# Tails of four tiles instead of three, and where the second half of their first tile stands, in one decoder layer

## The reference, cut to what matters

```python
y = sigmoid(gate_a) * y_a + sigmoid(gate_b) * y_b
h = y @ w_out                                   # output projection
x = layer_norm(alpha * x + h, ln1_g, ln1_b)
qry = x @ w_q                                   # query projection, then top-k over keys
...
hid = gelu(einsum('cd,chkd->chk', x, u_tab[expert]))
h = einsum('chk,chkd->cd', gate * hid, v_tab[expert])   # value projection
x = layer_norm(alpha * x + h, ln2_g, ln2_b)
```

## Time and profile before

| | |
|---|---|
| median of 3 runs | 1098.83 us (1098.72 to 1099.35) |
| profiled execution | 1099.08 us |
| its span | 1097.3 us |
| PE busy | 1081.6 us, 99% |
| DVE, ACT, POOL busy | 70%, 51%, 16% |
| DMA queue of SP | 181.30 MB, 48.7% of 16 engines |

### The profile page before, as it was taken

How to read it: one execution, slowest core, us unless ns; L and a number is a source line. 1 busy time by engine, 2 the same in 40 slices (tenths; PEclk the granted TensorE clock), 3 DMA queues, 4 the chain that set the end, 5 groups by cost and what they waited for, 6 DMA issues and landing times.

```text
span 1097.3 us, 19861 instructions
## 1 busy us (share of the span) xinstructions
PE 1081.6 (99%) x6760; PEld 969.3 (88%) x6760; DVE 773.4 (70%) x1403; ACT 559.2 (51%) x903; POOL 177.5 (16%) x118
## 2 busy tenths in 40 slices
PE   8999999999999999999999999999999999999996
PEld 6888888678999999999999999998888888888885
DVE  4457657387999868889998777765555555555556
ACT  4347544564344555555556545545554455455553
POOL 2040002203000002223334555520000000000001
PEclk9999999999999999999999999999999999999998
DMA  7554344253445554444444443445565655555553
GB/s 280 190 194 155 134 157 150 96 173 129 159 166 180 185 179 155 156 163 160 153 154 153 142 146 134 137 153 193 198 208 204 205 193 191 191 191 191 192 193 112
DMA packets 52711, 186.48 MB, mean 170 GB/s; under 512 B 6320, under 2 KB 6704, under 8 KB 52672
## 3 DMA queue, kind: packets, MB, share of 16 engines
q1 hardware_dynamic: 50864, 181.30, 48.7%
q0 software_dynamic: 944, 3.15, 0.8%
q10 hardware_dynamic: 864, 1.57, 0.4%
HBM read 184.94 MB, written 1.05 MB: 169 GB/s over the span
## 4 chain that ended last, share of the span: by engine, by line
PE 92%; DVE 3%; DMA 2%; ACT 2%; POOL 1%; issue 1%; POOLq 0%; SPq 0%; DVEq 0%; ACTq 0%
PE ps L1172 17%; PE ps L1174 17%; PE ps L1173 17%; PE ps L1499 10%; PE ps L1500 10%; PE ps L1501 10%; PE ps L1460 5%; DMA raw<-w_tiles_in 1%; PE ps L1224 1%; ACT whi L462 1%; DVE wlo L726 1%; PE ps L1426 1%; PE ps L1300 1%; PE ps L1311 0%; PE ps L1316 0%
## 5 line engine op out<-in xcount | busy, mean ns | idle before, releaser
L726 DVE TENSOR_TENSOR wlo<-raw,whi 128x1024 fp32r<-128x1024 f32 x341 | 421.4, 1237 | 258.7 <-ACT whi L462 256.6
L462 ACT ACTIVATE whi<-raw 128x1024 fp32r<-128x1024 f32 x343 | 363.2, 1060 | 303.9 <-DMA raw<-w_tiles_v 167.8
L1172 PE MATMUL ps<-ahi,whi 128*128 128x256 f32 x1152 | 332.5, 289 | 0.4 <-DVE alo L987 0.4
L1174 PE MATMUL ps<-ahi,wlo 128*128 128x256 f32 x1152 | 325.8, 283 | 0.0
L1173 PE MATMUL ps<-alo,whi 128*128 128x256 f32 x1152 | 325.7, 283 | 0.0
L1172 PEld LDWEIGHTS ps<-ahi,whi 128*128 128x128 f32 x1152 | 220.6, 191 | 0.6 <-issue 0.6
L1173 PEld LDWEIGHTS ps<-alo,whi 128*128 128x128 f32 x1152 | 220.8, 192 | 0.0
L1174 PEld LDWEIGHTS ps<-ahi,wlo 128*128 128x128 f32 x1152 | 220.5, 191 | 0.0
L1499 PE MATMUL ps<-whi,hhi 128*128 128x512 f32 x512 | 199.3, 389 | 0.9 <-DVE wlo L726 0.9
L1500 PE MATMUL ps<-wlo,hhi 128*128 128x512 f32 x512 | 199.2, 389 | 0.0
L1501 PE MATMUL ps<-whi,hlo 128*128 128x512 f32 x512 | 199.2, 389 | 0.0
(11 more groups left out here) (198 smaller groups left out, 922.8 us busy)
## 6 DMA issues: line engine op xcount, KB each, us to landing
raw<-w_tiles_u SPq DMA_DIRECT2D x128, 512.0 KB, 3.2
raw<-w_tiles_v SPq DMA_DIRECT2D x128, 512.0 KB, 3.2
raw<-w_tiles_in SPq DMA_DIRECT2D x63, 512.0 KB, 3.2
raw<-w_tiles_q SPq DMA_DIRECT2D x16, 512.0 KB, 3.2
raw<-w_tiles_out SPq DMA_DIRECT2D x8, 512.0 KB, 3.2
xraw<-xT ACTq DMA_DIRECT2D x4, 256.0 KB, 6.3
xt<-x POOLq DMA_DIRECT2D x1, 1024.0 KB, 7.8
raw<-w_tiles_in SPq DMA_DIRECT2D x2, 256.0 KB, 4.6
```

Source lines behind the costliest of these rows:

```text
L462: act.activation(whi[:, tile.slot, :], raw[:, tile.slot, :], ACT.Copy)\
L726: dve.tensor_tensor(wlo[:, tile.slot, :], raw[:, tile.slot, :], whi[:, tile.slot, :].bitcast(F32), ALU.subtract)\
L1172: pe.matmul(out, ah, bh, start=start, stop=False)
L1174: return pe.matmul(out, al, bh, start=False, stop=stop)
```

## The change

`TAIL` becomes 4. In both stages the tail thus has four tiles, whose t = 0 halves come first. Right before the last tile's t = 0, PE does both column halves of t = 1 of the tail's first tile and adds one to `tiles_used`. The loops over t = 1 behind it leave that tile out. In the output projection the wait for all of `act_split_lo` thereby stands in front of tile 4 instead of tile 5. In the value stage the loop for the tile that was between the register loop and the tail goes.

```diff
@@ -81,7 +81,7 @@
 GLA_DS, GLA_STATE, GLA_OUT, GLA_SSQ, GLA_VAR = (53, 54, 55), (54, 55, 56), (56, 57), (57, 58), (58, 59)
 GLA_SQRT, GLA_RMS = (59, 60), (60, 61)
 GATE_B, TIMES_GATE_B, GATE_A = 56, (57, 58), 60
-TAIL = 3
+TAIL = 4
 Y_TURN, Y_LATE = T_OUT - 1, 1
 
 BLK = 4
@@ -1376,13 +1376,15 @@
         pe.wait_ge(S["act_split_lo"], NS + 4)
         for k in range(TILES_OUT - TAIL, TILES_OUT):
             tile = Tile(T_OUT + k)
+            if k == TILES_OUT - 1:
+                out_half(Tile(T_OUT + TILES_OUT - TAIL), TILES_OUT - TAIL, 1).then_inc(S["tiles_used"], 1)
             tile_ready(tile)
             for half in range(2):
                 last = out_half(tile, k, 0, (half,))
                 if k == TILES_OUT - 1:
                     last.then_inc(S[("x1_bank", "half_done")[half]], 1)
         for half in range(2):
-            for k in range(TILES_OUT - TAIL, TILES_OUT):
+            for k in range(TILES_OUT - TAIL + 1, TILES_OUT):
                 last = out_half(Tile(T_OUT + k), k, 1, (half,))
                 if half == 1:
                     last.then_inc(S["tiles_used"], 1)
@@ -1518,18 +1520,16 @@
                 values_ready(tile)
                 values(tile, 0, False, False)
                 values(tile, 1, False, False).then_inc(S["tiles_used"], 1)
-        for m in range(T_END - 4, T_END - TAIL):
-            values_ready(Tile(m))
-            values(Tile(m), 0, False, False)
-            values(Tile(m), 1, False, False).then_inc(S["tiles_used"], 1)
         for m in range(T_END - TAIL, T_END):
+            if m == T_END - 1:
+                values(Tile(T_END - TAIL), 1, False, False).then_inc(S["tiles_used"], 1)
             values_ready(Tile(m))
             for half in range(2):
                 last = values(Tile(m), 0, False, m == T_END - 1, (half,))
                 if m == T_END - 1:
                     last.then_inc(S[("out_bank", "half_done")[half]], 1)
         for half in range(2):
-            for m in range(T_END - TAIL, T_END):
+            for m in range(T_END - TAIL + 1, T_END):
                 last = values(Tile(m), 1, False, m == T_END - 1, (half,))
                 if half == 1:
                     last.then_inc(S["tiles_used"], 1)
```

## The result

Over 12 runs of each, the changed kernel took 1101.35 us in the median (1101.12 to 1103.48) and the kernel before 1098.91 (1098.40 to 1100.31): ratio 1.0024, with a 95% interval of 1.0016 to 1.0032. The ratios in this document leave out two executions, one of the kernel before (1530.70 us) and one of `shift_one_tensor` (3345.89 us), whose granted clock was 0.65 and 0.32 on average.

What follows compares the result with a forecast made beforehand. PE was taken to bound the kernel, ending the chain for 92% of the span. The layer norm's +1.16 us, with the output projection's 0.14 inside it and the value stage at 0, gave 1100.0 us, range 1098.7 to 1101.8.

Steps and rivals of the forecast that it cites:

- Steps 1 and 2: Output projection: no wait for `alo`, cost 0; PE's 0.52 us stall goes from tile 7 to tile 5, sum +0.14 us.
- Step 3, the load, ACT's split and square root: First query tile: load issued 3.51 us later, at 247.00; ACT's split starts at 250.26, the square root at about 251.3.
- Step 3, POOL: First layer norm: POOL's split ends at 253.79, its multiplication follows at 253.85, 1.16 us later; 2.41 us was all the cover.
- Step 4: After the first layer norm: transposes start at 257.65 instead of 256.49; the layer norm gives +1.16 us in all.
- rival C: Whole kernel: the delay meets unseen slack, no visible change, +0.1 us, 1098.9; chance 0.08.
- Step 3, the spread: First query tile's load: landing in 3.1 us gives +1.05 in all, in 5.0 gives +2.9; 3.26 was taken.
- Step 5: Value stage: PE waits 0.4 us at the second last tile and as much less at the last; cost 0.
- D: Whole kernel: faster by over 0.2%, which would need 2.2 us back; chance 0.02.
- B: First query tile: the load lands late, up to 5.0 us, +2.9 us, 1101.7; chance 0.07.
- A: Gap before the query projection: PE's clock drops, 2.2 us lost, total +3.4, 1102.2; chance 0.07.

Runs made afterwards that it cites:

- shift_one_tensor: The changed kernel with DVE's shift step written as `tensor_scalar`, one tensor operand read from SBUF instead of two: 1100.38 against 1099.34 us for the kernel before, ratio 1.0010.
- pool_split_late: The kernel before with one wait added: POOL's split of the first query tile waits for DVE's variance; 1101.14 against 1099.26 us, ratio 1.0020.
- out_only: The changed kernel with the new value stage taken back, so the tail of four is in the output projection alone: 1102.0 against 1099.34 us for the kernel before, ratio 1.0023.
- pool_after_shift: The changed kernel with one wait added: POOL's split of the first query tile begins after DVE's shift step; 1101.34 against 1099.34 us for the kernel before.

## Why the prediction was right or wrong

- **The kind of error**: the number lies in the range, but the path to it was in part wrong, and that it lay there is luck.
- **Steps 1 and 2**: right to 0.01 us. No wait for `alo`; the stall of 0.52 us was given back as one of 0.65 at tile 5.
- **Step 3, the load, ACT's split and square root**: right to 0.1 us.
- **Step 3, POOL**: this is the step that failed. The prediction took POOL's split as work that stands only in POOL's own queue, with 2.41 us of cover, and named nobody else who would feel it. The description of the kernel before says likewise that semaphores are the only tie between the engines; they are not, since a running POOL instruction held one of DVE's for which every semaphore was there. The trace of before had 26 such rows, above. It said of ACT's scaling "0.6 us" late. But the split had moved onto the moment at which DVE's shift step is due, and the step was held for 2.0 us; ACT's scaling was 2.47 us late, and that and not POOL's queue set the end. `shift_one_tensor` takes this hold away and leaves the forecast loss (+1.04 us, forecast +1.16); `pool_split_late` makes the hold with load and square root on time and loses 1.9 us.
- **Step 4**: the shift went through whole, 2.46 us at the transposes and at the query projection, 2.4 in the medians. Nothing later absorbed it, so rival C (no visible change) was wrong. The second token half was held with the first, since DVE's next steps stand behind the shift step.
- **Step 3, the spread**: for a landing in 3.1 us the prediction says +1.05 in all; by its own terms it is 1.16 - 0.16 = 1.00.
- **Step 5**: 0 forecast, -0.2 us measured with an interval that holds 0. PE's wait came wholly at the second last tile (0.55 us) and not in part at the last, since that tile's load was quicker than before.
- **Rivals**: D did not occur. B (a late landing) did not; the load landed in 3.2 us. A was half right: the clock did not fall in the profile of the changed kernel, but it fell in that of `out_only` and in that of `pool_after_shift`. Its price, 2.2 us, was about 0.9 in `out_only`. Its condition, "only if one idle stretch of 1.5 us is enough", left out the second stretch, taken as 0.5 us and in fact 1.72, because the shift step was held. Transposes alone did not bring the clock down: it stayed at 1.00 through them before and after.
- The total lay in the range because B, another case that did not occur, had been priced at +2.9. The chance of 0.84 for "within 0.2%" was too high: the sum had taken every instruction on POOL and DVE to be as fast wherever it stood.

## What to carry to other kernels

When a step moves in time on one engine, list what the others run at its new place, the shortest instructions first. A view with least, median and greatest duration of a line shows which kinds are held (1203, 1225 and 2952 ns for DVE's split here). In this case a DVE step of 0.16 us in front of the whole chain was held for most of a POOL instruction of 2.4 us. A small DVE step that reads two tensors from SBUF of one element per partition can be written with the second as a per-partition scalar, which was not held here. And in a gap that is bridged by warming matmuls, look at what releases these, not only at how many they are.

## What the runs showed of the hardware

- DVE's two-tensor step on 128 x 1 took 0.42 to 2.13 us beside POOL's `tensor_tensor`, always until POOL's end; with a scalar operand 0.21. The steps that read one tensor from SBUF and one from PSUM (L943) took 0.67 to 0.69 us beside POOL's split as without it, and POOL's split took 2.35 to 2.41 in all cases. It had begun first in all of them; where a POOL `tensor_tensor` began second beside DVE's split, it was POOL that took longer (1.22 us for 0.74, in the trace of before).
- The granted clock fell to 0.50 after 2.07 us without a matmul in `pool_after_shift`, and in `out_only` during transposes, after 1.64 and 1.71 us idle with 14 matmuls between. With 1.49 and 1.72 us it stayed at 1.00 in the profile of the changed kernel, with 1.01 and 1.71 in that of `pool_split_late`. What decides between these was not tried further.
- One load of 512 KB on SP's queue, the last of the value stage, landed 3.65 us after its issue in the profile of before and 3.18 in that of the changed kernel.
